# Two stacked two-layer blocks on one core: one attention pipeline a layer, wide beta and gate rows, and a delta stage of five levels with substitution

## The reference, cut to what matters

```python
# layer 0: windowed attention, 12 query heads on 4 key heads, and 4 heads into a memory of 256 tokens
s = where(|t - s| <= 128, q k^T / 8 - slope * |t - s|, -inf);  p = softmax([s, sink]);  y_tok = p v
y_mem = softmax(qm mk^T / 8) mv
x = x + concatenate([y_tok, y_mem]) @ w_out[0]
# layer 1: neighbourhood attention, 12 heads of their own keys, on a grid of 8 x 64 tokens
s = where(column in window of 16, q k^T / 8 + rpb[dr, dc], -inf)          # rpb (12, 15, 31)
# layer 2: a causal convolution branch y_a and a gated delta rule with 4 heads of 128
beta = sigmoid(h @ w_beta);  g = -exp(a_log) * softplus(h @ w_alpha + dt_bias)
S_t = exp(g_t) (I - beta_t k_t k_t^T) S_{t-1} + beta_t k_t v_t^T;  o_t = S_t^T q_t
y_b = rms_norm(o, dn_norm_w) * silu(z)                                    # per head of 128
h = h + concatenate([y_a, y_b]) @ w_out
# layer 3: causal windowed attention with sinks, 16 query heads on 4 key heads, normed q and k
```

## Time and profile before

| what | us |
| --- | --- |
| time, median of 3 runs | 2709.09 |
| lowest and highest | 2707.14, 2709.68 |
| profiled execution: its span | 2705.2 |
| PE busy | 2589.5 (96%) |
| PE weight loads busy | 2245.8 (83%) |
| POOL busy | 1222.9 (45%) |
| ACT busy | 964.4 (36%) |
| DVE busy | 935.7 (35%) |

### The profile page before, as it was taken

How to read it: one execution, slowest core, us unless ns; L and a number is a source line. 1 busy time by engine, 2 the same in 40 slices (tenths; PEclk the granted TensorE clock), 3 DMA queues, 4 the chain that set the end, 5 groups by cost and what they waited for, 6 DMA issues and landing times.

```text
span 2705.2 us, 46485 instructions
## 1 busy us (share of the span) xinstructions
PE 2589.5 (96%) x16378; PEld 2245.8 (83%) x16378; DVE 935.7 (35%) x1714; ACT 964.4 (36%) x2169; POOL 1222.9 (45%) x1032
## 2 busy tenths in 40 slices
PE   7989999999998999999998888999999888999999
PEld 7767888888766888888998878999999766998897
DVE  4263221222153321226733443441432443442341
ACT  4384322232285322234223223321233465322231
POOL 4554444444573444444423544444444443444443
PEclk9999999999999999999988998999999999999999
DMA  4222222222240222222211001222222100222222
GB/s 166 82 48 70 93 103 83 93 101 86 90 80 24 93 96 94 89 105 90 86 63 47 1 16 55 91 99 82 86 100 79 40 25 26 92 93 101 86 99 95
DMA packets 80491, 212.96 MB, mean 79 GB/s; under 512 B 30336, under 2 KB 33024, under 8 KB 80384
## 3 DMA queue, kind: packets, MB, share of 16 engines
q1 hardware_dynamic: 80384, 211.56, 23.4%
HBM read 209.44 MB, written 2.10 MB: 78 GB/s over the span
## 4 chain that ended last, share of the span: by engine, by line
PE 90%; DVE 4%; ACT 3%; issue 2%; POOL 1%; DMA 0%; DVEq 0%; POOLq 0%; ACTq 0%; SPq 0%
PE ps L1238 76%; PE ps L1513 3%; PE ps L1426 2%; PE ps L1408 1%; DVE s_sb L1690 1%; PE ps L1357 1%; PE ps L1385 1%; PE ps L1370 1%; PE ps L1253 1%; ACT s_sb L915 1%; PE ps L1483 1%; POOL bias_sb L663 1%; DVE s_sb L1665 0%; PE ps L1433 0%; DVE y_sb L1665 0%
## 5 line engine op out<-in xcount | busy, mean ns | idle before, releaser
L575 POOL TENSOR_TENSOR w_lo<-raw,w_hi 128x512 fp32r<-128x512 f32 (+1 forms) x704 | 977.8, 1410 | 1175.4 <-ACT w_hi L816 1175.0
L816 ACT ACTIVATE w_hi<-raw 128x512 fp32r<-128x512 f32 (+1 forms) x704 | 426.9, 653 | 1341.6 <-PE ps L1238 1323.4
L1238 PE MATMUL ps<-h_hi,w_hi 128*128 128x512 f32 (+2 forms) x2992 | 855.0, 333 | 13.5 <-POOL h_lo L747 8.1
L1238 PE MATMUL ps<-h_lo,w_hi 128*128 128x512 f32 (+2 forms) x2992 | 853.0, 332 | 0.0
L1238 PE MATMUL ps<-h_hi,w_lo 128*128 128x512 f32 (+2 forms) x2992 | 851.1, 332 | 0.0
L1238 PEld LDWEIGHTS ps<-h_hi,w_hi 128*128 128x128 f32 x2992 | 511.1, 189 | 74.7 <-issue 15.0
L1238 PEld LDWEIGHTS ps<-h_lo,w_hi 128*128 128x128 f32 x2992 | 507.0, 189 | 55.1 <-issue 1.0
L1238 PEld LDWEIGHTS ps<-h_hi,w_lo 128*128 128x128 f32 x2992 | 507.5, 189 | 54.2
L1238 PE MATMUL ps<-act_lo,w_hi 128*128 128x512 f32 (+1 forms) x880 | 280.5, 351 | 0.0
L1238 PE MATMUL ps<-act_hi,w_lo 128*128 128x512 f32 (+1 forms) x880 | 279.8, 350 | 0.0
L1238 PE MATMUL ps<-act_hi,w_hi 128*128 128x512 f32 (+1 forms) x880 | 278.8, 349 | 0.0
(11 more groups left out here) (248 smaller groups left out, 2625.7 us busy)
## 6 DMA issues: line engine op xcount, KB each, us to landing
raw<-slabs_d SPq DMA_DIRECT2D x288, 512.0 KB, 3.2
raw<-slabs_d SPq DMA_DIRECT2D x64, 704.0 KB, 4.0
rpb_raw<-rpb_d SPq DMA_DIRECT2D x24, 224.0 KB, 5.0
bias_sb<-alibi_d SPq DMA_DIRECT2D x6, 384.0 KB, 3.8
...
mem_in<-mem_d SPq DMA_DIRECT2D x1, 1024.0 KB, 8.6
...
```

The costliest lines, as they stand in the source:

```text
L575: nc.gpsimd.tensor_tensor(w_lo[:, s, a * P:b * P], raw[:, s, a * P:b * P], w_hi[:, s, a * P:b * P].bitcast(f32), ALU.subtract).then_inc(lo ...
L816: nc.scalar.activation(w_hi[:, s, a * P:b * P], raw[:, s, a * P:b * P], ACT.Copy)\
L1238: last = nc.tensor.matmul(ps[:, s * 2 * BANK + po:s * 2 * BANK + po + n], w[:, s, wk], a[:, k, to:to + n], start=(k == 0 and w is w_hi and ...
```

## The change

It does the following.

- **Layers 0 and 1.** One stage `tiles` a layer in place of two stages `att`: 8 tiles (6 and 2 for the memory), 32 pairs in one loop (`TilePair`, `over_tile_pairs`, `attend_tiles`). The division is made once per tile, 512 tokens wide: DVE takes the reciprocals of 128x8 and spreads them itself, PE transposes four of them together (`reciprocals`), ACT moves and rounds 512 columns (`y_tile`), DVE multiplies once, POOL makes one low part. The rpb bias is laid out with its mask on the host and loaded like the alibi bias, one transfer of 128 x 2 x 896 values (917 KB) a tile, two buffers; POOL's `mask` is gone. Slab 0 of the out stage waits for `y_lo_ready` by tile, as its steps read them.
- **Even stage.** The beta and gate rows are 32 matmuls, weights stationary (16 columns, high and low part side by side, with the high part of the activations; 8 with the low), 264 tokens wide. ACT copies them to `ba_rows`; after the first of the 8 slabs five small matmuls with `ba_sum` add the parts and turn them to tokens on the partitions. ACT's `gates` follows the norm of tile 0.
- **Delta stage.** Five pieces a round, at most five levels. The last doubling becomes a substitution in the tail: `vt` solves the top 64 rows, `yb` multiplies them by `a_t`'s lower left block, `res2` adds that on DVE, `vb` solves the bottom 64 rows. Two state buffers. The heads' norm is made by chunk, two rounds behind (`head` for `fin`), and the stage `tn` "head" is gone; there is one more round. Of the out slabs 0 and 1, steps 0 to 3 (48 matmuls, on the convolution's half) stand in PE's program in rounds 5 and 6 (`slab_part`), and the rest behind the rounds.
- **Layer 3.** The spread of reciprocals moves from ACT to a copy on DVE.

The diff, cut to its core:

```diff
-    att(nt=6, blocks=a_blocks, bias="alibi", sink=0, qt=0, kt=6, group=3, y=0, layer=0)
-    att(nt=2, blocks=m_blocks, bias=None, sink=None, qt=8, kt=0, group=1, y=6, layer=0)
+    tiles(blocks=a_blocks, bias="alibi", sink=0, kt=6, group=3, layer=0, mem_qt=8)
...
 def levels_of(c):
-    return [s for s in range(1, LEVELS) if (1 << s) < CHUNKS[c][1]]
+    return [s for s in range(1, LEVELS - 1) if (1 << s) < CHUNKS[c][1]]
...
-    pre = dict(pe=["rows", "dcol", "kk", "kq", "at", "xm"], dve=["dcol", "d", "dlast", "a1", "a", "qk"],
-               act=["gb", "erow", "elast", "abs", "e", "at", "xm"], pool=["em", "first", "xt"])
-    tail = dict(pe=["vks", "kt", "vn", "o", "s"], dve=["res", "kd", "s1", "s"], act=["vn", "o"], pool=["ke", "qe"])
+        "tail": dict(pe=["vks", "kt", "vt", "yb", "vb", "s", "o"], dve=["res", "kd", "s1", "res2", "s"],
+                     act=["vt", "vn", "o"], pool=["ke", "qe"]),
+        "head": dict(pe=["ms"], dve=["norm", "gate", "lo"], act=["sq", "ln", "exp", "hi"]),
+    }
+    halved, carried = ("yb", "vb", "res2", "vn"), ("kt", "kd", "s1", "s")
...
+                width = 3 * P if st.bias == "alibi" else BIAS_W
+                if not isinstance(i, int) or i >= 2:
+                    sp.wait_ge(max_ready, 2 * ((i - 1) * 4 + st.pair0))
+                if not isinstance(i, int) or i >= 1:
+                    sp.wait_ge(bias_full[st.bias], i * 16)
+                sp.dma_start(bias_sb[:, i % 2, :, 0:width], d[st.bias][i]).then_inc(bias_full[st.bias], 16)
...
-                def spread(p):
-
-                    act.wait_ge(inv_ready, p.count + 1)
-                    if counted(p.count - 1):
-                        act.wait_ge(pv_done, p.count - 1)
-                    nc.scalar.activation(p_rec[0:p.nq, p.slot, :].rearrange("p (h n) -> p h n", h=2),
-                                         p_inv[0:p.nq, p.slot, :].unsqueeze(2).to_broadcast([p.nq, 2, HD]),
-                                         ACT.Copy).then_inc(rec_ready, 1)
...
+                def values(p):
+                    if p.b == 0:
+                        pe.wait_ge(v_staged, p.tile + (st.tile0 + 1))
+                        if p.after(8):
+                            pe.wait_ge(y_ready, p.tile + (st.unit0 - 1))
+                    for h in range(2):
+                        pe.wait_ge(pt_ready[h], p.count + 1)
+                    value_products(p, bank(6 + p.tile_slot)[:, p.b * P:(p.b + 1) * P]).then_inc(pv_done, 1)
+
+                def reciprocals(tile, s):
+
+                    pe.wait_ge(inv_ready, tile + (st.unit0 + 1))
+                    pe.wait_ge(y_moved, tile + (st.unit0 + 1))
+                    for b in range(4):
+                        last = nc.tensor.transpose(bank(6 + s)[:, b * P:(b + 1) * P], p_rec[:, s, b, :], ident)
+                    last.then_inc(rec_done, 1)
+
+                def step(p):
+                    scores(p)
+                    if p.after(2):
+                        turn(p.back(2))
+                    if p.after(3):
+                        values(p.back(3))
+                    if p.b == 0 and p.after(8):
+                        reciprocals(p.tile - 2, p.tile_slot)
...
+                for k in range(DT):
+                    for m, a in ((16, hi), (8, lo)):
+                        for c, (_, to, n) in enumerate(chunks(2)):
+                            last = nc.tensor.matmul(acc(2, 2)[0:m, c, :], w_ba_parts[:, k, 0:m], a[:, k, to:to + n],
+                                                    start=(k == 0 and a is hi), stop=(k == DT - 1 and a is lo))
+                last.then_inc(ba_summed, 1)
+                    if j == 0:
+                        pe.wait_ge(ba_moved, 1)
+                        for c, (t0, n) in enumerate(CHUNKS):
+                            last = nc.tensor.matmul(bank(4)[0:n, ba_bank][:, 8 * c:8 * c + 8], ba_rows[0:16, t0:t0 + n],
+                                                    ba_sum[0:16, :], start=True, stop=True)
+                        last.then_inc(ba_done, 1)
...
+                for w, a in ((w_hi, hi), (w_hi, lo), (w_lo, hi)):
+                    for po, to, n in chunks(2):
+                        last = nc.tensor.matmul(
+                            ps[:, s * 2 * BANK + po:s * 2 * BANK + po + n], w[:, s, wk], a[:, k, to:to + n],
+                            start=(k == 0 and w is w_hi and a is hi), stop=(k == DT - 1 and w is w_lo))
+                if k == DT - 1:
+                    last.then_inc(pe_done, 1)
...
 
                 for s in range(RING):
                     pe.wait_ge(acc_free[s], st.slab0 // 2)
-                for here, _, old, new, i in rounds():
+                for here, mid, old, new, fin, i in rounds():
                     if here:
                         first_product(here, here.levels[i])
                     if old:
                         tail(old, i)
                     if here:
                         second_products(here, here.levels[i])
+                    if fin and i == 1:
+                        head(fin, old)
                     if new:
                         pre(new, i)
+                    if old and old.c == LAST and i < 4:
+                        slab_part(st, 0, i)
+                    if fin and fin.c == LAST and i < 4:
+                        slab_part(st, 1, i)
+                Chunk(LAST).after(pe, "head", "dve", "lo")
+                for s in range(RING):
+                    for k in range(DT // 2, DT):
+                        slab_part(st, s, k)
...
+                    if st.blk == 1:
+                        slab(q0, 0, st.blk, *outputs(st), made=y_lo_ready, at=st.unit0 - TILES)
+                        slab(q0, 1, st.blk, *outputs(st))
+                        many(q0 + 1, DT // 2 - 1, st.blk, *outputs(st))
+                        continue
...
+                def invert(tile, s):
+
+                    wait(p_ready, 2 * (st.pair0 + 4 * tile + 4))
+                    if tile >= 2:
+                        wait(rec_done, st.unit0 + tile - 1)
+                    recip(p_inv[:, s, :, :], p_sum[:, s, :, :])
+                    copy(p_rec[:, s, :, :].rearrange("p b (h n) -> p b h n", h=2),
+                         p_inv[:, s, :, :].unsqueeze(3).to_broadcast([P, 4, 2, HD])).then_inc(inv_ready, 1)
+
+                def normalise(tile, s):
+                    wait(rec_done, st.unit0 + tile + 1)
+                    y = y_tile[st.h][:, s, :]
+                    tt(y, y, bank(6 + s), ALU.mult).then_inc(y_ready, 1)
+
+                for g in range(TILES // 2):
+                    for pos in range(8):
+                        p = TilePair(st, g, pos)
+                        scores(p)
+                        if p.b == 0 and p.tile >= 1:
+                            invert(p.tile - 1, 1 - p.tile_slot)
+                        if p.b == 1 and p.tile >= 2:
```

And in the delta stage, ACT and DVE:

```diff
+                def head(k, i):
+                    done, q = d_sem["head", "act"], head_q[:, :, 0:k.n]
+                    if i == 0:
+                        k.after(act, "tail", "act", "o")
+                        if k.c:
+                            Chunk(k.c - 1).after(act, "head", "dve", "norm")
+                        nc.scalar.activation(q, qkv[:, 8:12, k.tok], ACT.Square).then_inc(done, 1)
+                    if i == 1:
+                        k.after(act, "head", "pe", "ms")
+                        nc.scalar.activation(q, quad(k.ms_bank, k.n), ACT.Ln, scale=1.0 / P, bias=eps_col).then_inc(done, 1)
+                    if i == 2:
+                        k.after(act, "head", "act", "ln")
+                        nc.scalar.activation(q, q, ACT.Exp, scale=-0.5).then_inc(done, 1)
+                    if i == 3:
+                        k.after(act, "head", "dve", "gate")
+                        nc.scalar.activation(h_hi[st.h][:, 4:8, k.tok], qkv[:, 8:12, k.tok], ACT.Copy).then_inc(done, 1)
 
                 act.wait_ge(gate_made, 1)
                 spread_gate(Chunk(0))
-                for here, _, old, new, i in rounds():
+                for here, mid, old, new, fin, i in rounds():
...
+                def head(k, i):
+                    done, o = d_sem["head", "dve"], qkv[:, 8:12, k.tok]
                     if i == 2:
-                        after(k, "tail", "pe", "kt")
-                        tt(k_dec[0:n, :, :], quad(2, P)[0:n], per_token(k.elast[0:n, :], P), ALU.mult).then_inc(done, 1)
+                        after(k, "head", "act", "exp")
+                        stt(o, o, dn_gain, head_q[:, :, 0:k.n], ALU.mult, ALU.mult).then_inc(done, 1)
+                        tt(o, o, zed[:, :, k.tok], ALU.mult).then_inc(done, 1)
                     if i == 4:
-                        after(k, "tail", "pe", "o")
-                        tt(state[:, :, :], state[:, :, :], per_token(k.erow[:, :, n - 1], P), ALU.mult).then_inc(done, 1)
-                    if i == 5:
-                        after(k, "tail", "pe", "s")
```

(4 more changed lines are left out.)

944 lines of the change are left out of this document (474 added, 470 removed).

## The result

The changed kernel takes 2689.08 us in the median of five runs (2683.83 to 2692.25), the kernel before 2709.09. The ratio is 0.9919 with a 95% interval of 0.9899 to 0.9938: 20 us less where 66 were forecast, and outside the range of 2628 to 2660. The profiled execution has a span of 2690.4 us against 2705.2, 14.8 less; it is the slowest of the five.

What follows compares the result with a forecast made beforehand. TensorE, nine tenths of the chain, was taken as the bound. Layer 1 -16.4, layer 0 -10.9, beta and gate rows -16.7, delta -22.1, layer 3 0 sum to -66.1: 2709.1 becomes 2643 us, range 2628 to 2660.

Steps and rivals of the forecast that it cites:

- Rows of beta and gate: Before layer 2's slabs: 32 wide matmuls replace 120 narrow entries, 28.4 us becomes 11.7, -16.7 us.
- a pair is 3.20 - 0.26 + 0.13 = 3.07: Layer 1's attention: one reciprocal transpose less a pair, four unbroken per tile instead; with mask waits gone, -8.2 us.
- The memory stretch: Layer 1, last bias pair to last memory pair: one pipeline without drain, 22.0 us instead of 27.5, -5.5.
- The end of the stage: Layer 1, last scores to first out slab: slab waits only for needed head tiles, 8.9 us becomes 7.2, -1.7.
- The slabs' start: Layer 1's first nine out slabs lose 1.8 us after the idle stretch; less idle gives back -1.0.
- the walk of the orders: Delta rounds, stepping through both instruction orders: full round stays 29.2 us; round 1 -3.0, round 2 -1.2, round 4 -0.8.
- about 0.9 longer: Delta piece 1: ACT's Square and DVE's k_dec queue ahead, lengthening the wait by about 0.9 us.
- ACT's spread becomes a DVE copy ... 0, within 2 either way: Layer 3: reciprocals' spread moves to DVE, the rest issued as before; no change, within 2 us.
- The one given .18: Rival, delta: DVE's head norm, gate and low part contend with POOL, 1.07 us more each, +16, 2659 us; chance .18.
- The late bias tile: Rival, layer 1: the 917 KB bias transfer lands late and tiles wait; at 31 us late, 2717 us; chance .03.
- the sixth: Rival: stages don't overlap as written, slab parts sit on the chain, gain and loss cancel; 2709 us; chance .02.
- the first rival: The forecast itself, whole kernel: 2643 us, own range 2634 to 2652, allowing +3.9 for slow-clocked row matmuls; chance .55.

Runs made afterwards that it cites:

- the kernel with three edits: Changed kernel with values moved one pair earlier, Square behind the level's copy and k_dec behind dlast, layer 3's spread on ACT; median 2661.67 us, ratio 0.9830.

## Why the prediction was wrong

**Rows of beta and gate: right.** 32 matmuls took 3.86 us (3.9 forecast) at the full clock, the stage 11.9 instead of 28.4 (11.7 forecast). The term held within 0.2.

**Layers 0 and 1: the step that failed was "a pair is 3.20 - 0.26 + 0.13 = 3.07", with "nothing is between them".** The four transposes' work was 0.55 us a tile, near the 0.5 taken. Left out was their wait. The change added a condition, that ACT has moved the values, and in the order of the engines ACT's move stood behind the exponentials of a pair, and these behind its copies of a turn that TensorE makes in the very step that ends with the transposes. It cost 8.5 us in layer 1 and 9.3 in layer 0 (11.4 and 10.1 over the whole stages), and layer 1's last 19 us ran at a granted clock of 0.73, where it was 0.95 before and 1.00 with the order mended. With that one order mended layer 1's stretch came out at 58.3 us, the forecast's own figure, so the work in it had been counted rightly. Layer 0 then takes 2.40 us a pair (131.14 to 176.67 us for 19) where 2.28 were forecast and 2.46 stood before, with waits of 0.2 to 0.5 us for DVE's maximum. DVE's work was not the reason: reciprocal, copy and product took 0.20, 0.43 and 0.69 us a tile, 1.32 where 1.85 had been taken. My reading, which no run tests, is that these fall on single pairs, and an average over the tile hides that. The memory stretch was under-sized by 2.6 us (24.6 for 22.0), all of it in the steps over the switch, which were taken as one pair of 3.07 and two of 2.65 and took 4.22, 3.78 and 3.29. The end of the stage was under-sized by 1.3 us (8.5 for 7.2). The slabs' start gained 1.8 us a layer, more than the 1.0 taken.

**Delta: the walk of the orders was right within 0.6 us a round; the step that failed was to price the longer stop, "about 0.9 longer", at its own length, without the clock.** Forecast were 30.7, 28.0 and 29.2 us for the rounds 1 to 3 (33.7 and twice 29.2 before, less 3.0, 1.2 and 0). With the change's own program they took 30.8, 28.2 and 29.8 in the execution where the clock held, and 34.5, 31.4 and 31.4 in the profiled one. The prediction named the longer stop, 1.62 plus about 0.9, and it measured 2.34; it did not ask what a stop of that length does to the granted clock. The end took 25.9 us from 1595.98 to 1621.85, against 24.9: the chain up to the last 48 matmuls 18.25 instead of 19.0, and these 7.62 instead of 5.9, since they began at the lower clock. Up to the feed-forward net it gave 17.8 us, against 17.1. Round 4 gave nothing instead of -0.8.

**Layer 3: the step that failed was "ACT's spread becomes a DVE copy ... 0, within 2 either way".** The copy's own price was right: the tiles take 20.67 us instead of 20.38. But the turn of each pair waits for DVE's normalise (7.5 us in three tiles; before, 2.1 for DVE and 3.3 for ACT), the copy stands before it, and behind the longer gaps the clock was granted at half: 15.9 us more in this term, and 20.3 more for layer 3 in the kernel before with this edit alone. A wait was costed at its own length. What stays open is how much of it is chance, since the kernel with three edits, with the spread on ACT, took 644.5, 648.2 and 667.9 us in three profiles.

**The rivals.** The one given .18, DVE's head instructions meeting POOL's, did not occur but for one small instruction. Gate and low part of the chunk of 16 tokens, and POOL's instruction beside the latter; then norm, gate and low part of a full chunk, with POOL's first instruction behind a gap:

```profile
1531.96 0.23 DVE L1761 TENSOR_TENSOR qkv<-qkv,zed 128x64 f32<-128x64 f32 x1 [0.46 <-issue]
...
1538.94 1.27 POOL L752 TENSOR_TENSOR a_lv<-a_t,dn_cst 128x512 f32<-128x512 f32 x1
...
1539.41 0.89 DVE L1761 TENSOR_TENSOR h_lo<-qkv,h_hi 128x64 fp32r<-128x64 f32 x1
...
1562.06 0.75 DVE L1756 SCALAR_TENSOR_TENSOR qkv<-qkv,vec,head_q 128x512 f32<-128x512 f32 x1
1562.90 0.69 DVE L1761 TENSOR_TENSOR qkv<-qkv,zed 128x512 f32<-128x512 f32 x1
...
1564.74 1.28 POOL L752 TENSOR_TENSOR x_t<-a_t,dn_cst 128x512 f32<-128x512 f32 x1 [7.58 <-ACT a_t L1168]
...
1570.82 0.79 DVE L1761 TENSOR_TENSOR h_lo<-qkv,h_hi 128x512 fp32r<-128x512 f32 x1
```

0.75, 0.69 and 0.79 us, as costed and far from the 1.76 of the earlier trace rows. The walk had POOL idle there, and for norm and gate the rows agree: POOL stood idle for 7.58 us up to 1564.74. The Trainium skill, "GPSIMD Engine Reference" (specifications), names contention for such instructions. The low part of 64 columns fits it: beside a running POOL it took 0.89 us, where the gate of the same size, with POOL idle, took 0.23. It is 0.7 us of the 16 that the rival had. The late bias tile did not occur either (5.2 us from issue to landing). The time itself, 2689, lay between the 2659 of the third rival and the 2709 of the sixth (.02), where no rival stood; the clock, which made most of it together with ACT's order, was in the first rival for the 32 matmuls alone, where it didn't fall, and in none at the places where it did.
